# GLA's level of 16 tokens as block products: one constant of a 2-layer hybrid decoder kernel

## What is computed

```python
def gla_chunked(q, k, v, log_a, s0):
    '''S_t = diag(alpha_t) S_{t-1} + k_t v_t^T, o_t = q_t S_t, evaluated chunkwise (exact).'''
    ...
    def step(s, blk):
        qc, kc, vc, gc = blk
        b = jnp.cumsum(gc, axis=1)
        diff = b[:, :, None] - b[:, None, :]
        w = jnp.exp(jnp.where(causal[None, :, :, None, None], diff, -jnp.inf))
        scores = jnp.einsum('bihd,bjhd,bijhd->bhij', qc, kc, w)
        o = (jnp.einsum('bhij,bjhe->bihe', scores, vc)
             + jnp.einsum('bihd,bhde->bihe', qc * jnp.exp(b), s))
```

## Time and profile before

| | |
|---|---|
| median of 3 runs | 2465.09 us (2463.67 to 2467.01) |
| the profiled execution, its time | 2467.69 us |
| its span, first to last instruction | 2465.9 us |
| TensorE busy, of the span | 2430.1 us, 99% |
| VectorE, GpSimd, ScalarE busy | 56%, 41%, 32% |
| granted TensorE clock, mean | 0.995 of 2.4 GHz |
| GLA's stage, from the first to the last score product | 1210.8 to 1608.2 us |

### The profile page before, as it was taken

One profiled execution on the slowest core, in us unless ns is written; L12 is line 12 of the kernel. 1 busy time (PEld: TensorE's weight loads), 2 busy tenths in 40 slices (PEclk: granted clock), 3 DMA queues, 4 the chain that ended last, 5 costly groups with the idle time before them and its releaser, 6 DMA issues. The chain is left out here.

```text
span 2465.9 us, 40868 instructions
## 1 busy us (share of the span) xinstructions
PE 2430.1 (99%) x15934; PEld 2383.1 (97%) x15934; DVE 1388.4 (56%) x2082; ACT 792.5 (32%) x1244; POOL 1003.2 (41%) x751
## 2 busy tenths in 40 slices
PE   8999999999999999999999999999999999999997
PEld 8999999999999999999999999999999999999997
DVE  6974366345545545567666666556345545445576
ACT  4711442222223223223344454442222122122233
POOL 2343124364554555473101111134364564464571
PEclk9999999999999999999999999999999999999999
DMA  4123031111111111111311111131111111111112
GB/s 149 35 63 89 25 125 45 43 44 43 52 52 42 46 51 43 52 52 41 120 42 58 51 45 55 34 126 49 46 44 43 53 44 43 52 48 39 52 53 80
DMA packets 40010, 140.09 MB, mean 57 GB/s; under 512 B 6208, under 2 KB 9920, under 8 KB 38560
## 3 DMA queue, kind: packets, MB, share of 16 engines
q1 hardware_dynamic: 32192, 104.55, 13.0%
q10 hardware_dynamic: 7648, 33.04, 3.7%
HBM read 120.46 MB, written 14.88 MB: 55 GB/s over the span
## 5 line engine op out<-in xcount | busy, mean ns | idle before, releaser
L716 PE MATMUL PS<-RB,WH 128*128 128x384 f32 (+1 forms) x4368 | 1085.6, 330 | 6.8 <-issue 6.8
L716 PEld LDWEIGHTS PS<-RB,WH 128*128 128x128 f32 x4368 | 770.8, 189 | 15.6 <-issue 12.7
L716 PE MATMUL PS<-RA,WH 128*128 128x272 f32 (+2 forms) x3520 | 770.5, 309 | 11.7 <-DVE RA L1809 10.4
L716 PE MATMUL PS<-RB,WL 128*128 128x384 f32 (+1 forms) x2232 | 730.6, 327 | 0.0
L716 PEld LDWEIGHTS PS<-RA,WH 128*128 128x128 f32 x3520 | 588.1, 188 | 16.2 <-issue 11.8
L716 PE MATMUL PS<-RA,WL 128*128 128x272 f32 (+2 forms) x1760 | 541.1, 307 | 0.0
L622 POOL TENSOR_TENSOR WH<-WR,FEW 128x1024 fp32r<-128x1024 f32 x106 | 204.8, 1932 | 775.4 <-PE PS L716 750.6
L716 PEld LDWEIGHTS PS<-RB,WL 128*128 128x128 f32 x2232 | 420.3, 188 | 0.0
L716 PEld LDWEIGHTS PS<-RA,WL 128*128 128x128 f32 x1760 | 331.2, 188 | 0.0
L1908 DVE TENSOR_TENSOR X<-PS,X 128x544 f32<-128x544 f32 x280 | 202.5, 724 | 203.7 <-PE PS L716 203.7
L1849 DVE SCALAR_TENSOR_TENSOR RAW<-PS,RS 128x384 f32<-128x384 f32 (+1 forms) x192 | 97.2, 532 | 350.0 <-PE PS L716 321.4
(11 more groups left out here) (225 smaller groups left out, 2375.7 us busy)
## 6 DMA issues: line engine op xcount, KB each, us to landing
WR<-ws SPq DMA_DIRECT2D x189, 512.0 KB, 3.3
X<-xT ACTq DMA_DIRECT2D x8, 544.0 KB, 8.0
EB<-xT ACTq DMA_DIRECT2D x8, 544.0 KB, 5.6
x_spill<-X ACTq DMA_DIRECT2D x1, 4352.0 KB, 15.2
EB<-x_spill ACTq DMA_DIRECT2D x8, 544.0 KB, 7.0
GA<-st_gla ACTq DMA_DIRECT2D x4, 1024.0 KB, 5.1
glas_o<-GA ACTq DMA_DIRECT2D x4, 1024.0 KB, 3.9
yT<-X SPq DMA_DIRECT2D x16, 208.0 KB, 1.9
```

Source lines behind the costliest of these rows:

```text
L716: return nc.tensor.matmul(out, lhsT, rhs, start=start, stop=stop, skip_group_check=True)
```

## The change

One constant is changed:

```diff
-FINE = 5
+FINE = 4
```

## The result

| | before | changed |
|---|---|---|
| median | 2465.32 us (16 runs, 2463.67 to 2469.08) | 2473.66 us (16 runs, 2468.48 to 2480.84) |
| ratio to before, 95% interval | | 1.0033 (1.0024 to 1.0041) |
| the profiled execution, its time | 2467.69 us | 2472.91 us |
| its span | 2465.9 us | 2471.1 us |
| mean granted TensorE clock | 0.995 | 0.993 |

The change made the kernel 0.33% slower, 8.3 us in the medians and 5.2 us between the two profiled spans. I had predicted 2459.8 us.

A forecast was written before the change was run, and what follows sets the result against it. TensorE's stream, busy 99% of the span, was taken as the bound. Products saving 5.0 us and VectorE's copies 0.3 made 5.3 us less than 2465.1: 2459.8 us, range 2457.4 to 2463.9.

The forecast's parts named there:

- What bounds the kernel: Whole kernel: TensorE's products fill 99% of the span, so time changes through its stream or not at all.
- Added: eight records, 0.05; net 0.16 a place: GLA's stage, TensorE: eight 16-column records add 0.05 us, the removed wide product frees 0.21; 31 places give 5.0 us.
- Moved: the hole of 0.13: TensorE's idle 0.13 us between levels 5 and 4 moves to between level 4 and the projection's load; net nothing.
- VectorE: a copy less brings the last chunks' levels forward, 0.3 us: Last chunks of heads 1 and 2: one masked copy less shortens TensorE's wait by 0.15 us each, 0.3 in all.
- rival E: GLA's stage: TensorE arrives earlier, waits for VectorE's levels grow, at most some 2 us returned; 2461.8 us, chance 0.06.
- The sum: 5.0 + 0.3 = 5.3 us less: profiled execution 2467.69 to 2462.4, median 2465.1 to 2459.8 us.
- B: Level 4's eight records are handed out at a fixed 0.02 us each; gain 1.9 us, 2463.2 us, chance 0.14.
- C: Level 4's four narrow products run one after another, 0.19 us lost a place; 2471.2 us, chance 0.07.
- D: A second 0.13 us hole opens between levels 5 and 4, at 32 to 16 columns; 2463.9 us, chance 0.06.
- The clock: TensorE's half-clock stretch in head 0's last chunk costs 1.7 us; one more or less after a shift is chance.

The follow-up runs named there:

- e1: Changed kernel plus 16 long-met waits (8 instructions) on TensorE's queue just ahead of the second MLP's loop; 2463.56 us, ratio 0.9991 to before.
- e3: Changed kernel plus 8 do-nothing instructions on each of TensorE's and VectorE's queues ahead of the second MLP's loop; 2460.54 us, ratio 0.9981 to before.
- e2: Changed kernel plus 8 do-nothing instructions on VectorE's queue only, ahead of its second MLP loop; 2471.07 us, ratio 1.0025 to before.
- e4: Kernel before plus 8 long-met waits (4 instructions) in each of 32 places on TensorE, 128 in all; 2477.46 us, ratio 1.0049.
- e6: Kernel before with TensorE's loops over the MLP turns written out for both layers, so no jumps back; 2456.58 us, ratio 0.9965.

## Why the prediction was wrong

**What bounds the kernel: right, and not carried through.** "A time can then change through TensorE's stream, or not at all." It did change there, but I looked for TensorE's holes in GLA's stage alone. The 2.2 us at 1948.96 were in the trace of before, with "issue" as their reason, and so were 7.0 us of such waits over the whole run; I gave them no thought.

**Added: eight records, 0.05; net 0.16 a place: right.** Measured 0.18, 31 x 0.18 = 5.6 us. The eight records added some 0.06. **Moved: the hole of 0.13, counted at nothing: right to 0.03,** it is now some 0.10.

**VectorE: a copy less brings the last chunks' levels forward, 0.3 us: wrong in sign.** Both come earlier at head 2's last chunk, but TensorE by 4.43 us (1459.06 to 1454.63) and VectorE's level by 4.24 (1459.89 to 1455.65), so the wait grew by the rest, 0.19; over the stage the waits in the products grew by 0.4 us. That is rival E, at a fifth of its price. The stage as a whole gained 5.0 us, where the two terms made 5.3. That the sum of the stage came so close is in part luck: 5.6 instead of 5.0, and -0.4 instead of +0.3.

**The sum: the step that failed.** "5.0 + 0.3 = 5.3 us less. ... so the same execution would take 2462.4" takes for granted that everything behind the stage keeps its time. I priced the new records by how long they run, and not by the room they take in the program. The change adds 384 instructions ahead of a loop, and the two jumps back of that loop went from 2.2 and 2.0 us to 5.1 and 5.5: +6.4, and +1.9 of half clock behind them. The missing term is +8.3 us, larger than the whole gain.

**The rivals.** B (a floor per record), C (one after another, the only slower one) and D (a second hole) are all refuted by the one place read closely: 0.30 us for twelve records, no hole between 32 and 16 columns. C's 2471.2 us lies near the result, by accident: its mechanism is absent. Slower by over 0.2% was given 0.08, all of it tied to the products and a clock stretch. With the jumps priced, the forecast would have had two cases: a head that stays inside a block (e1, e3), and one that meets an edge (as measured).

**The clock.** "One more or less of them after a shift of some us is chance" held within the stage. Behind a long gap it isn't: all six (changed, e2, e4) were followed by a stretch of 6.8 us. Behind a short one it goes with the gap's length, but not in every case: 3.41 us behind six of the seven gaps of 2.04 to 2.20 us, and none behind the fifteen of 1.52 to 1.98.

## What to carry to other kernels

Before costing any edit, look for the places where the bounding engine stands still with "issue" as the reason, and ask whether they are jumps back of a loop; count how many instructions the edit adds ahead of each, because that moves the loop's head over the edges of the fetched blocks. If the time moves and the timeline at the edit doesn't explain it, line up the two traces and put some long-met waits ahead of the loop (here 8 instructions took the loss away, and 128 in the kernel before brought it). Where a loop has few turns, writing it out is worth more than many a clever edit: here 8.7 us, against 3.5 for the products.

## What the runs showed of the hardware

**A jump back on TensorE costs 1.5 to 2.2 us, or 4.9 to 5.5.** These are distances from the last product ahead of the jump to the first behind it. The short price was seen 22 times, at the jumps of both layers' loops, with one 16 KB packet on the instruction queue (0.9 to 1.4 us) and some 1.5 us from its end to the first instruction; the long one six times (changed, e2, e4), with two packets one after the other and the loop's first instruction between them. The Trainium skill states the rule, in "Runtime: NRT & Kernel Launch", section "Instruction fetch mechanics": instructions come in 16 KiB blocks of 256, prefetched in sequence only, and a taken branch to outside the pages at hand waits for a fetch. The trace agrees: packets of 16 KB, some 257 instructions for each in e6, and a fetch at every jump back. The section also says that crossing a block's edge is mostly hidden, and that holds in straight code (0.2 us of "issue" waits in e6's products on line 716 over 126 packets); right behind a jump it doesn't hold, with 3 us for an edge.

**The clock answers to such a gap.** Behind gaps of 5 us the granted clock was 0.50, that is 1.2 GHz, for 6.8 us; behind the 22 short ones it was so for 3.4 us in six cases (gaps of 2.04 to 2.20 us) and not at all in the others (1.52 to 1.98 us, and one of 2.08).

**Narrow products in different strips are nearly free.** Eight fp32 records of 16 columns at partitions 0, 32, 64 and 96 lengthened the busy stretch of level 5 by 0.04 us, and the last of them starts some 0.06 us behind level 5's last. The overhead of some 60 cycles for each matmul, which the prediction cited from the Trainium skill against the change, isn't seen in them: by its estimate of 25 ns a record they would have added 0.20 us.
